# Paired attentions: the second head's turned copy is put ahead of the next pair's second maximum on VectorE

## The reference

```python
def gqa_attend(q, k, v, bias=None, sink=None):
    s = jnp.einsum("bqhgd,bkhd->bhgqk", q, k) * ATTN_SCALE
    if bias is not None:
        s = s + bias
    ...                                  # a sink is one more column
    p = jax.nn.softmax(s, axis=-1)
    return jnp.einsum("bhgqk,bkhd->bqhgd", p, v)
```

## Time and profile before

| | |
|---|---|
| median of 3 runs | 1794.69 us (1794.65 to 1797.04) |
| the profiled execution's own time | 1799.19 us |
| its span, first to last instruction | 1797.9 us |
| PE busy | 1724.9 us, 96% |
| DVE busy | 990.7 us, 55% |
| ACT busy | 742.1 us, 41% |
| mean granted TensorE clock | 0.99 |
| units of A and B, about | 1140 to 1331 us |
| units of D, about | 1620 to 1687 us |

### The profile page before, as it was taken

The page is one execution under the profiler, slowest core; times in us unless marked ns, Lnnn a source line. Parts: engine busy times, 40 slices in busy tenths (PEclk is TensorE's granted clock), DMA queues, the critical chain, the costliest instruction groups (busy, mean ns, idle before and its releaser), DMA issues.

```text
span 1797.9 us, 24836 instructions
## 1 busy us (share of the span) xinstructions
PE 1724.9 (96%) x9530; PEld 1386.2 (77%) x9530; DVE 990.7 (55%) x2000; ACT 742.1 (41%) x1465; POOL 641.6 (36%) x272
## 2 busy tenths in 40 slices
PE   8999999889999999999999999999889999999997
PEld 6889666678888888888788876655568888896776
DVE  4797545533233455555792415566643667975553
ACT  5222344552333454344324432466753225225553
POOL 3877222253334454544646122100003233521132
PEclk9999999999999999999999999999999999999999
DMA  8656221132324233333662221100002442321021
GB/s 236 188 141 188 65 71 48 48 98 80 93 70 141 82 89 99 94 94 99 187 194 88 66 90 36 36 1 1 2 1 59 134 127 74 88 68 47 14 89 53
DMA packets 255155, 156.30 MB, mean 87 GB/s; under 512 B 6017, under 2 KB 250942, under 8 KB 255038
## 3 DMA queue, kind: packets, MB, share of 16 engines
q1 hardware_dynamic: 251518, 147.12, 28.1%
q10 hardware_dynamic: 3520, 7.60, 1.2%
HBM read 152.60 MB, written 2.10 MB: 86 GB/s over the span
## 4 chain that ended last, share of the span: by engine, by line
PE 83%; DVE 7%; issue 4%; ACT 3%; POOL 1%; DMA 1%; ACTq 0%; DVEq 0%; SPq 0%
PE ps L783 66%; PE ps L2417 3%; PE ps L2428 2%; PE ps L2447 2%; POOL w_lo L764 1%; PE ps L1567 1%; DVE mod_sums L1500 1%; PE ps L1551 1%; PE ps L1515 1%; DVE mod_sums_odd L1500 1%; DVE probs L2519 1%; PE ps L789 1%; PE ps L1559 1%; PE ps L2453 1%; PE ps L2165 1%
## 5 line engine op out<-in xcount | busy, mean ns | idle before, releaser
L764 POOL TENSOR_TENSOR w_lo<-w_raw,w_hi 128x1024 fp32r<-128x1024 f32 (+1 forms) x220 | 586.2, 2669 | 1080.9 <-ACT w_hi L705 1080.4
L783 PE MATMUL ps<-h_hi,w_lo 128*128 128x512 f32 x1088 | 433.6, 399 | 10.5 <-DVE h_lo L1102 2.9
L783 PE MATMUL ps<-h_hi,w_hi 128*128 128x512 f32 x1088 | 424.5, 390 | 0.0
L783 PE MATMUL ps<-h_lo,w_hi 128*128 128x512 f32 x1088 | 424.2, 390 | 0.0
L783 PEld LDWEIGHTS ps<-h_hi,w_lo 128*128 128x128 f32 x1088 | 204.5, 188 | 59.8 <-issue 6.0
L705 ACT ACTIVATE w_hi<-w_raw 128x1024 fp32r<-128x1024 f32 (+1 forms) x220 | 228.6, 1044 | 37.1 <-PE ps L783 20.6
L783 PEld LDWEIGHTS ps<-h_hi,w_hi 128*128 128x128 f32 x1088 | 204.3, 188 | 43.7
L783 PEld LDWEIGHTS ps<-h_lo,w_hi 128*128 128x128 f32 x1088 | 204.6, 188 | 41.2 <-issue 1.4
L2502 ACT ACTIVATE probs<-probs,small 128x512 f32<-128x512 f32 (+3 forms) x128 | 93.7, 732 | 24.0 <-DVE small L2519 21.2
L2428 PE MATMUL ps<-ident,probs 128*128 128x128 f32 x528 | 85.8, 287 | 15.2 <-ACT probsT L2485 7.0
L2428 PEld LDWEIGHTS ps<-ident,probs 128*128 128x128 f32 x528 | 56.5, 142 | 54.4 <-issue 30.3
(11 more groups left out here) (425 smaller groups left out, 3313.6 us busy)
## 6 DMA issues: line engine op xcount, KB each, us to landing
w_raw<-in_w_in SPq DMA_DIRECT2D x56, 512.0 KB, 5.2
mod_raw<-in_mod_w SPq DMA_DIRECT2D x24, 1024.0 KB, 5.9
w_raw<-in_w_up SPq DMA_DIRECT2D x44, 512.0 KB, 3.8
w_raw<-in_od_w_in SPq DMA_DIRECT2D x28, 512.0 KB, 3.8
w_raw<-in_ev_w_in SPq DMA_DIRECT2D x20, 512.0 KB, 3.8
w_raw<-in_w_down SPq DMA_DIRECT2D x16, 512.0 KB, 4.3
w_raw<-in_w_mem_kv SPq DMA_DIRECT2D x8, 512.0 KB, 3.9
w_raw<-in_w_attn_branch SPq DMA_DIRECT2D x8, 512.0 KB, 4.0
```

What stands on the lines that cost most here:

```text
L764: POOL.tensor_tensor(wlo[:, p, 0:n], raw[:, p, 0:n], f(whi[:, p, 0:n]), ALU.subtract).then_inc(*chunk_lo.by(c))
L783: ins = PE.matmul(out, l, r, start=first and n == 0, stop=last and n == 2)
```

## The change

In each step of `dve_pairs` VectorE copies the turned tiles (p-1, 1) before it takes the maximum (p, 1). No instruction, buffer or semaphore is added or removed, and TensorE's, ScalarE's and GpSimd's streams stay as they are. All three attentions use this function.

```diff
                 DVE.reciprocal(inv, total).then_inc(*p_inverted.by(x_, p - 1))
+            if 1 <= p <= n:
+                copy(p - 1, 1)
             if p < n:
                 dve_maximum(x_, p, us[p], 1, probs)
-            if 1 <= p <= n:
-                copy(p - 1, 1)
             yield
         dve_out(n // 2 - 1, x_, us)
```

## The result

The changed kernel takes 1893.95 us (median of 4 runs, 1891.99 to 1902.8), the kernel before 1795.84 beside it. The ratio is 1.0554, with a 95% interval of 1.0525 to 1.0584: 98 us slower. The forecast was 1874 (1862 to 1892). Its direction and mechanism hold, its size does not: the time lies 2 us above the range and 20 above the forecast.

The account below looks back on a forecast made before the run. TensorE, busy 96% of the span, was taken to bound the kernel. 72.3 us over the steps, 6 from ScalarE and 1 from the clock made 79 on the median of 1794.7: about 1874 us, range 1862 to 1892.

Parts of the forecast that it names:

- Turning, copy and maximum in a row: In each step of the attentions, TensorE's turning, VectorE's copy and maximum, then the next scores run serially, no longer side by side.
- The sum over the steps, 72.3: Maxima and copies newly exposed over 62 steps of A, B and D, after corrections for cover and overlaps: 72.3 us.
- ScalarE's 6 us: Tiles come later behind ScalarE's late exponential and copy: 8 groups of A and B at 0.53, 12 D steps at 0.15.
- the price of one step: In A's long steps, 1.47 us from copy start to scores plus 0.11 for the later copy start; 4.13 us becomes 5.71.
- D's steps 1 and 8 hidden: Ahead of D's units 2 and 9, layer-norm sums of 3.60 and 3.88 us cover the delay: 2.2 us less.
- Step 2 of A in full, through ScalarE: TensorE there waits for ScalarE's copy of B's values, behind an exponential late by the same 1.5 us; counted in full.
- What the clock adds, 1 us: TensorE's holes in A, B and D cost a little under one clock loss, 1 us; bounds 0 and 7 losses (12 us).
- the prediction's own sign of being wrong: Wrong if A's long steps take under 5.4 or over 6.0 us, low clock exceeds some 10 us, or later stages give time back.
- The rival of ten to twenty losses: The clock falls some ten to twenty times in the changed stages, giving 1891 to 1908 us; chance 8%.
- The evidence that the clock would hold: From 388 to 398 TensorE was busy 6.36 of 10 us and kept 2.4 GHz; new A steps, about 4.0 of 5.7.
- The basis: Profiled execution of 1799.19 us, 4.5 above the median; with 79 us added 1878.5, or about 1874 against the median.
- Stages behind give nothing back, no gain from the earlier copy: Losses in A and B move everything behind them; bank 4 freed earlier can't pay. Rival of a faster kernel, 1789 us: chance 1%.

Follow-up runs that it names:

- run 2: VectorE waits for the turned tiles (p-1, 1) before the maximum (p, 1) but copies after it, against the kernel before: 1859.53 us, ratio 1.0353.
- experiments 1 and 3: 1: new order in the odd layer (D) alone, against the kernel before, 1816.48 us; 3: changed kernel plus 220 idle TensorE matmuls in the even layer, 1882.16 us.
- experiment 10: Kernel before, old VectorE order, with ScalarE's copy ahead of its exponential only before short context units and in step 47: 1793.41 us, ratio 0.9982.
- run 8: Kernel before with, in the odd layer, the new order, own score banks from unit 5 and ScalarE's copy before its exponential: 1807.22 us in one run.

## Why the prediction was right in kind and too small

- **Turning, copy and maximum in a row.** Right, by the row from 1186.98 on and by run 2.
- **The sum over the steps, 72.3, and ScalarE's 6 us.** Right. Together 78.3 us. By steps, ScalarE's part shows as 0.54 us above the price of one step in A's steps 16 and 17, as 0.67 in B's 28 and 29 (0.53 a group was forecast), and as 0.12 in each of D's steps 12 to 14 (0.15). The steps in which the clock fell give the comparison: A 10 took 1.36 us more than A 16, A 20 1.56 more than A 14, B 26 1.39 more than B 32, B 28 and its three fellows 1.43 more than with the hole filled, the end of the list 1.45. That is 11.5 us. Step 3 took 0.8 us more than a long step's price; no run has the new order without the fall there, so this part is an estimate. The 74.0 us of A and B less these 12.3 are 61.7, and D alone, with as much time at the low clock as before, cost 16.9: 78.6 against 78.3. The forecast's own split (60 without the clock, and 17) leaves 1.3 us of its sum unplaced.
- **D's steps 1 and 8 hidden.** Right. Step 1 took 7.40 us before and after. Step 8 took 6.84 us in experiments 1 and 3 with the new order and in experiment 10 with the old; in the profiled executions of the kernel before and the changed one (7.09 and 7.86) the clock fell inside it.
- **Step 2 of A in full, through ScalarE.** Right: 6.23 became 7.71, 1.48 for 1.5.
- **What the clock adds, 1 us.** This term was mis-sized, and it is the step that failed: it measured 12.3 us in A and B and 1.6 in D, 13.9 us. The prediction judged the clock by the mean of a step (4.0 of 5.7 us) and took "a little under one" loss. The time at the low clock grew from 3.4 to 34.1 us in A and B and from 6.8 to 10.2 in D, ten stretches of 3.4 us more, at about 1.4 us each; my bound of 7 was too low. By the prediction's own sign of being wrong, more than some 10 us at the low clock, it was wrong. The rival of ten to twenty losses, which had 8%, gives the measured time (1891 to 1908). What decides where a fall comes stays open: steps of the same length lost the clock (A 20) and kept it (A 14), and a stretch busy for 1.25 of 3.60 us kept it.
- **The evidence that the clock would hold.** The prediction leaned on the stretch from 388 to 398, busy for 64% and at 2.4 GHz. This was the luck of one execution. That stretch is ahead of the change and the same in all kernels, and in ten of the other twelve profiled executions the clock fell in it or just behind it, between 394 and 401. The changed kernel's, with the share of TensorE before the fall and the stretch behind it:

```profile
388.00:398.00 10.00, 6.47 (x38) 4.83 (x36) 6.64 (x8) 4.83 (x7) 1.82 (x1) 0.99 0.17 52
397.70:401.10 3.40, 3.04 (x12) 2.78 (x13) 1.89 (x4) 1.94 (x4) 0.00 (x0) 0.50 0.02 5
```

- **The basis.** I took off 4.5 us, by which the profiled execution stood above the median. The profiled execution of the changed kernel, 1893.47 us, does not stand above its median. Against its own basis the forecast was 1878.5, 15.0 too low; the other 5 us of the miss are this subtraction. The 15.0 us are 12.9 of the clock in these stages, 0.3 of the sum and 1.8 outside the stages. In the profiled execution before, D held 3.4 us more at the low clock than in experiment 10 (77.0 against 75.4 us), which is a part of it.
- **Stages behind give nothing back, no gain from the earlier copy.** Right, by the 278.0 and 278.1 us between the stages.
- **What I had not seen.** That the output product's chain hangs on the same maximum in odd steps (run 8), and that ScalarE's late copy was on TensorE's path in the old order as well.

What stays open is also where the clock falls in another run: the steps named here are those of one profiled execution.

## What to carry to other kernels

An instruction that waits for the last work of a step should stand behind everything on its engine that the next step needs at once; ask what is queued behind a moved wait and price it from the durations of a single step, which here gave 78 us to within one. When a busy TensorE gets regular holes, its busy share by the mean of a step doesn't tell whether the clock holds, and one execution in which it held doesn't either: look at several profiled executions, and count what some ten falls would cost. Before more buffers are spent on one wait, follow every path that leaves the late instruction: here three had nearly the same length; cutting one showed nothing, cutting two freed the even steps alone.

## What the runs showed of the hardware that was not expected

- More work on TensorE made the kernel faster: 220 idle matmuls took 12 us off (1893.95 to 1882.16), by keeping the clock at 0.99 instead of 0.94.
- The falls came at the same place in four groups of B (steps 28, 34, 40, 46), each for 3.4 us and at a cost of 1.4 us, where 3.4 us at half the clock would cost 1.7 without any wait (an estimate).
- A TensorE that is busy all the time can lose the clock: within 32 one-column matmuls (3.88 us) or just behind them it fell to 1.2 GHz for 3.4 or 6.8 us in every profiled execution.
- The same instructions lost the clock in one execution and kept it in another: the stretch from 388 to 401 us, ahead of every change, in ten of thirteen.
- Most steps repeat to 0.02 us from run to run where the clock holds, so single steps of one profile can carry an experiment that the whole time can't: a change of 0.6 us in seven steps was plain in the timeline and just clear of noise in eleven runs.
